# A fifth pair of gate tiles in the projection stage, and late outputs copied behind the last maxima

## The reference

```
h = rms_norm(x, g_mix)
proj = h @ w_in            # q, k, v of mixer A; q, k, v of mixer B; 2 x 1024 gate logits
y_a = chunk_band_relbias_attention(qa, ka, va, rel_table) @ w_branch_a   # 8 heads, 576-key band
y_b = sliding_window_sink_gqa(rope(qb), rope(kb), vb, sinks) @ w_branch_b # 8 heads, 128-key window
g_a, g_b = split(sigmoid(gate_logits + b_gate))
x = x + (g_a * y_a + g_b * y_b) @ w_out
x = x + (silu(h2 @ w_g) * (h2 @ w_u)) @ w_down,  h2 = rms_norm(x, g_ffn)
```

## Time and profile before

| what | value |
|---|---|
| median of three timed executions | 2600.32 us (2600.06 to 2602.14) |
| the profiled execution's own time | 2601.09 us |
| its span, first to last instruction | 2599.3 us |
| PE busy | 2562.3 us, 99% of the span |
| DVE busy | 1827.1 us, 70% |
| ACT busy | 1040.9 us, 40% |
| POOL busy | 288.7 us, 11% |
| granted TensorE clock, mean | 0.998 |
| HBM | 128 GB/s over the span |

### The profile page before, as it was taken

One profiled execution on the slowest core, in us unless ns is written; L12 is line 12 of the kernel. 1 busy time (PEld: TensorE's weight loads), 2 busy tenths in 40 slices (PEclk: granted clock), 3 DMA queues, 4 the chain that ended last, 5 costly groups with the idle time before them and its releaser, 6 DMA issues. The chain is left out here.

```text
span 2599.3 us, 35484 instructions
## 1 busy us (share of the span) xinstructions
PE 2562.3 (99%) x12822; PEld 2096.4 (81%) x12822; DVE 1827.1 (70%) x3321; ACT 1040.9 (40%) x2051; POOL 288.7 (11%) x442
## 2 busy tenths in 40 slices
PE   7999999999999999999999999999999999999998
PEld 6888777788888888888878887777888888888886
DVE  8766555554888777768996664555459778776687
ACT  6222456532533333344642224664235333333444
POOL 0000232344000000000000002224430000000000
PEclk9999999999999999999999999999999999999999
DMA  4323543353132233395423344424422233225843
GB/s 151 127 102 114 181 135 116 120 178 128 57 118 101 90 114 113 99 277 168 154 102 117 111 139 155 141 87 167 154 109 86 88 111 122 83 104 164 262 118 126
DMA packets 200333, 336.93 MB, mean 130 GB/s; under 512 B 18672, under 2 KB 79968, under 8 KB 200160
## 3 DMA queue, kind: packets, MB, share of 16 engines
q1 hardware_dynamic: 191936, 311.47, 35.8%
q10 hardware_dynamic: 8224, 23.20, 2.6%
HBM read 240.76 MB, written 92.92 MB: 128 GB/s over the span
## 5 line engine op out<-in xcount | busy, mean ns | idle before, releaser
L1397 PE MATMUL ps<-op_hi,up_hi 128*128 128x512 f32 x1232 | 480.5, 390 | 2.5 <-DVE third_sum L2970 2.5
L1399 PE MATMUL ps<-op_hi,up_lo 128*128 128x512 f32 x1232 | 480.0, 390 | 0.0
L1398 PE MATMUL ps<-op_lo,up_hi 128*128 128x512 f32 x1232 | 479.9, 390 | 0.0
L1397 PE MATMUL ps<-in_hi,up_hi 128*128 128x512 f32 x728 | 285.4, 392 | 3.3 <-DVE up_lo L2469 2.1
L1398 PE MATMUL ps<-in_lo,up_hi 128*128 128x512 f32 x728 | 284.1, 390 | 0.0
L1399 PE MATMUL ps<-in_hi,up_lo 128*128 128x512 f32 x728 | 284.0, 390 | 0.0
L1397 PEld LDWEIGHTS ps<-op_hi,up_hi 128*128 128x128 f32 x1232 | 231.4, 188 | 50.9 <-issue 3.3
L1399 PEld LDWEIGHTS ps<-op_hi,up_lo 128*128 128x128 f32 x1232 | 231.4, 188 | 48.2
L1398 PEld LDWEIGHTS ps<-op_lo,up_hi 128*128 128x128 f32 x1232 | 231.5, 188 | 47.5
L2069 ACT ACTIVATE up_hi<-up_raw 128x512 fp32r<-128x512 f32 x252 | 158.1, 630 | 277.7 <-PE ps L1399 271.6
L1350 POOL CAST w_hi<-w_raw 128x256 fp32r<-128x256 f32 x184 | 82.6, 491 | 1451.4 <-DMA w_raw<-w_lin 1216.4
(11 more groups left out here) (253 smaller groups left out, 4776.6 us busy)
## 6 DMA issues: line engine op xcount, KB each, us to landing
up_raw<-w_gu SPq DMA_DIRECT2D x42, 1024.0 KB, 4.9
act_raw<-ff_saved SPq DMA_DIRECT2D x154, 256.0 KB, 2.7
w_quarter<-w_lin SPq DMA_DIRECT2D x52, 512.0 KB, 4.3
w_raw<-w_lin SPq DMA_DIRECT2D x48, 512.0 KB, 4.4
ff_saved<-ff_block SPq DMA_DIRECT2D x88, 256.0 KB, 2.0
ff_saved<-ff_mix SPq DMA_DIRECT2D x66, 256.0 KB, 2.0
gated<-gates_saved SPq DMA_DIRECT2D x32, 512.0 KB, 4.3
dn<-w_dn_a SPq DMA_DIRECT2D x48, 256.0 KB, 4.0
```

What stands on the lines that cost most here:

```text
L1397: pe.matmul(out, w1, x1, start=first, stop=False, skip_group_check=True)
L1398: pe.matmul(out, w1, x0, start=False, stop=False, skip_group_check=True)
L1399: return pe.matmul(out, w0, x1, start=False, stop=last, skip_group_check=True)
```

## The change

There are five edits, and the diff shows them all.

1. `IN_GATES` is 5. A fourteenth pair is projected, and `GATE_TILES` falls from 8 to 6, so the fill has 96 steps instead of 128.
2. `FILL_A` and `FILL_B` place 72 steps among the runs where 104 stood. The 8 in front and the 16 behind stay.
3. At the end of the attention DVE no longer takes the outputs and the inverse at s = 125. It takes the maxima of units 126 and 127 first, then sums and inverts, then copies the inverse (`take_inverse`), multiplies (`scale_last`), and copies the four outputs (`take_heads`).
4. The unit of that step gets a name, `HELD`.
5. POOL's `split` of the first branch tile also waits until `scale_last` is done.

```
-IN_GATES = 4
+IN_GATES = 5
-FILL_A = ((8, 4, 4, 2, 2, 2, 2, 0),) + ((2, 2, 2, 1, 1, 1, 1, 0),) * (GROUPS - 1)
-FILL_B = ((8, 6),) * (GROUPS - 1) + ((4, 4),)
+FILL_A = ((8, 4, 2, 0, 2, 0, 0, 0),) + ((2, 2, 0, 0, 1, 0, 1, 0),) * (GROUPS - 1)
+FILL_B = ((5, 5),) * (GROUPS - 1) + ((4, 4),)
...
-    return LAST_UNIT + 4 if LAST_UNIT - EIGHT <= u < LAST_UNIT else run_end(run_end(u) + 1) + 1
+    return HELD if LAST_UNIT - EIGHT <= u < LAST_UNIT else run_end(run_end(u) + 1) + 1
...
+HELD = LAST_UNIT + 4
...
                 if t == GATE_TILES:
                     pool.wait_ge(o_hi_ready, L * (KT + 1) + 1)
+                    pool.wait_ge(inverse_step, (L + 1) * (EIGHTS + 1))
...
                         if after == EIGHTS - 1:
+                            take_inverse(L, SPREAD_EIGHTS - 1)
                             scale_last(L)
+                            for u in weighed_in(HELD):
+                                take_heads(L, u)
                     if s < UNITS:
                         row_max(L, s)
-                    for eight in inverses_at(s, 1):
-                        take_inverse(L, eight)
-                    for u in weighed_in(s - 1):
-                        take_heads(L, u)
+                    if s != HELD + 1:
+                        for eight in inverses_at(s, 1):
+                            take_inverse(L, eight)
+                        for u in weighed_in(s - 1):
+                            take_heads(L, u)
```

## The result

The changed kernel takes 2608.93 us (median of 8 runs, 2606.76 to 2611.39) against 2600.83 (8 runs, 2600.06 to 2603.02): a ratio of 1.0029, 95% interval 1.0020 to 1.0038, 0.2 to 0.4% slower. The forecast was 2608.0. The span grew from 2599.3 to 2607.6 us, the clock's mean stayed at 0.998.

The account below looks back on a forecast made before the run. PE's list was taken to bound attention, DVE's chain almost level. Per layer 9.68 us kept less 2.72 won, +13.9 for two, tail -6.7: +7.2, put at 2608.0 us; likeliest case 2605 to 2612, 8 in 10 within 2603 to 2614.

Parts of the forecast that it names:

- p = 2, three runs: Groups 1 to 3, two steps out: DVE's chain keeps 1.12 of 1.36 us per run, 1.00 without one operation's excess.
- p = 3, three runs: Groups 1 to 3, one step out: the chain nearly equals the run, so 0.67 of 0.68 us is kept each.
- p = 5, three runs: Groups 1 to 3, one step out: 0.12 us of 0.68 is kept per run.
- group 0: Kept there per layer: 0.57 us at p = 3, 0.41 in the first B run, 0.12 at p = 5; sum 1.10.
- three meetings: A half's first step waits for the previous half's bank to be scaled: 0.95 us each, 2.85 a layer.
- kept in all: Removed fill time not given back in a layer's attention: 5.73 + 1.10 + 2.85 = 9.68 us.
- tail: Attention's end: PE's waits go in both layers (5.1 us), and layer 0's slow clock (1.6): -6.7 us.
- POOL on every chain: Rotary operations at p = 2 and p = 3 run beside POOL more often: +15 us, 2616; chance 0.06.
- PE's work decides: Attention runs: DVE catches up, waits at p = 2 and p = 3 dissolve: 2588 us, faster; chance 0.07.
- Part of the waits: Attention runs: DVE's list advances, only the halves' waits come in full, half the rest: some 2602 us; chance 0.12.
- The tail doesn't do what it says: Attention's end: `scale_last` comes later for an unseen reason and PE still waits: +13.9 us, 2614; chance 0.04.
- The clock falls again: Short new waits at p = 2 and p = 3 bring half-clock stretches in three groups, two layers: +9.6 us, 2617; chance 0.05.

Follow-up runs that it names:

- e3: Changed kernel with two fill steps given back at p = 2 of groups 1 to 3 and all B runs at (4, 4): 2598.84 us, ratio 0.9984 to the kernel before.
- e5: Changed kernel with DVE's rotary operations behind the last maximum of their run, from group 0's B runs on: 2600.42 us, ratio 0.9993 to the kernel before.
- e4: Kernel before with 6 and 8 fill steps instead of 8 and 6 in the B runs of groups 0 to 2: 2612.49 us, ratio 1.0034.
- e6: The kernel of e1 without edit 5 (POOL's wait): 2595.40 us, ratio 0.9973 to the kernel before.
- e10: e7 with a sixth projected pair and no fill steps in the B runs: 2629.86 us, ratio 1.0106 to the kernel before.
- e1: Kernel before with edits 3 to 5 alone (four projected gate pairs, old fill tables): 2594.35 us, ratio 0.9970.
- e8: Changed kernel with e7's A table, B at (4, 4) in all groups and e5's order of rotary operations: 2593.41 us, ratio 0.9967 to the kernel before.
- e7: Changed kernel with its 72 fill steps placed by other A and B tables, no halves meeting in a run: 2590.78 us, ratio 0.9959 to the kernel before.
- e2: Changed kernel without edits 3 to 5 (five projected pairs and new tables alone): 2617.07 us, ratio 1.0056 to the kernel before.

## Why the prediction was right, step by step

The path was right, and most terms within a few tenths of a us. Per layer, from the run lengths (layer 0, layer 1):

| term | predicted | measured |
|---|---|---|
| p = 2, three runs | 3.36 | 3.0, 3.0 |
| p = 3, three runs | 2.0 | 1.8, 1.6 |
| p = 5, three runs | 0.36 | 1.0, 0.85 |
| group 0 | 1.10 | 1.9, 1.3 |
| three meetings | 2.85 | 3.4, 3.4 |
| kept in all | 9.68 | 11.1, 10.2 |
| tail | -4.5, -2.2 | -4.7, -2.5 |

- **What DVE's chain keeps.** Shown by e3 (fill back, loss gone) and e5 (chain shorter by 0.6, run shorter by 0.60). For p = 2 the value without POOL's excess (1.00) was the right one, six times of six. At p = 3 five of the six runs are 3.30 to 3.32 us, as worked out, and one is 3.76 beside POOL. But the prediction took one place for all: in four of the six the run had been 3.55 to 3.64 before and not 3.31, so less of the step was kept there (0.40 to 0.44 without POOL).
- **p = 5 and group 0** were mis-sized. In group 3 POOL's scaling fell beside the rotary operation of p = 5, and that run keeps 0.71 and 0.60 instead of 0.12:

```profile
459.25 1.26 DVE L2737 TENSOR_TENSOR swapped<-swapped,rope 128x512 f32<-128x512 f32 x1
```
```profile
459.23 0.73 POOL L675 TENSOR_TENSOR x_sb<-x_sb,inverse_rows 128x256 f32<-128x256 f32 x1 [7.93 <-DMA inverse_rows<-inverses_saved]
```

The third rival ("POOL on every chain") set this price at the six runs p = 2 and p = 3 of groups 1 to 3. It fell at three places a layer, 0.3 to 0.6 us each: p = 5 of group 3 and the first B run of group 0 in both layers (the latter 7.93 us in layer 0 against the chain's 7.44), with p = 3 of group 0 in layer 0 and p = 3 of group 1 in layer 1. The two operations above start 0.02 us apart, and DVE's takes 1.26 us where 0.69 is its time alone, while POOL's keeps its 0.73. The attentions of the changed kernel have 14 places in which POOL's scaling and a rotary operation of DVE overlap, and they are alike: the one that started first took its time alone (0.67 to 0.74), and the second ended up to 0.15 us before the first one's end plus its own time alone, whichever engine it was. A shared rate would have slowed both, so the rows show one waiting for the other. The Trainium skill, "SBUF — State Buffer", section "SBUF: two separate sides", has it so: whichever starts first holds the shared ports for its whole instruction, and the other is blocked. The trace agrees but for that 0.15 us.
- **Meetings.** 1.12 to 1.17 each for 0.95: the handoff back to PE took 0.15 where I took 0.05, and the restart of PE's row of matmuls 0.1. e4 shows that they cost 0.3 to 0.5 us more where DVE is late.
- **The fourteenth pair** took its 19.04 us. But the first stage grew by only 292.67 - 275.19 = 17.5 us; why is not shown, and in the kernels with five pairs that stage's end lies between 292.05 and 294.83 in single executions. The attentions gave 1.6 us less back than forecast, and the first projection asked for 1.6 us less, so the two cancelled in the sum. The span grew by 8.3 us for a sum of 7.2; the other 1.1 us lie outside these stages, 1.0 of it behind the second attention, where the prediction had nothing. Part of the closeness of 2608.0 to 2608.93 is luck.
- **The tail.** No wait, and no slow clock, as forecast. PE came to the transposes at 486.72, and DVE had ended at 485.08:

```profile
483.67 1.41 DVE L2797 TENSOR_TENSOR probs<-inverse,probs 128x256 f32<-128x256 f32 x4
```

The forecast left open whether the four would take 3.01 or 1.4; they took 1.41, also without POOL's wait (e6), so edit 5 is not the reason: the new order alone keeps the split behind them.
- **The rivals.** "PE's work decides" is refuted by the waits in the changed kernel and by e3 and e10. "Part of the waits" did not come: p = 2 and the meetings kept their terms in full. "The tail doesn't do what it says" is out by e1. "The clock falls again" did not occur in the changed kernel, where no new wait is over 1.1 us and both attentions stayed at 1.00. But the argument against it, that one wait of 2.24 us had kept the clock, was weak: in e8 it fell behind a wait of 2.45 us, and in e10 behind waits of 1.99 and 1.75 us.

## What to carry to other kernels

Fill is worth its time only above the chain that it covers: before taking fill out, write for each run the time from its first matmul to the handoff that frees the next one, and take steps only down to that length. The same 72 steps cost 18 us more or less by where they stood. And compare with the other parts alone: most of what e7 gains over the kernel before, e1 gains without a fifth pair.

When an instruction is moved, ask for each buffer that it frees what waits for it, and what stands behind that in the same list. In e8 a rotary operation moved out of DVE's chain freed its buffer later, the loads into it held up the queue engine's list, and a transfer behind them came too late for DVE.

## What was not expected of the hardware

- The clock after a wait: 2.89 us in the kernel before was followed by 0.50, 2.92 in layer 0 of e2 by 1.00, 2.94 in its layer 1 by 0.66 over the same 3.4 us. In group 1 of e10, waits of 1.99 and 1.75 us in neighbouring runs were followed by 0.52 in one layer and by 1.00 in the other. The length alone does not decide it; why it fell in one and not in the other stays open.
- A handoff from DVE to PE took 0.05 us behind an accumulator's read-out and 0.15 behind the scaling of a bank.
- Where POOL's scaling and a rotary operation of DVE overlap, the first to start lost nothing and the second paid the whole, up to 0.6 us, whichever engine it was.
